# Full-size matmuls in a convolution made of Fourier transforms, and another order of its steps on TensorE and VectorE

## The reference

```
def conformer_conv(x, w_pw1, b_pw1, w_dw, b_dw, ln_g, ln_b, w_pw2, b_pw2):
    h = x @ w_pw1 + b_pw1                      # 1024 -> 2048
    a, gate = jnp.split(h, 2, axis=-1)
    h = a * jax.nn.sigmoid(gate)
    h = conv_general_dilated(h, w_dw, padding=[(30, 0)], feature_group_count=1024) + b_dw   # 31 taps, causal
    h = jax.nn.silu(layer_norm(h, ln_g, ln_b))
    return h @ w_pw2 + b_pw2                   # 1024 -> 1024
```

## Time and profile before

| | before |
|---|---|
| median of 3 runs | 1293.32 us (1292.26 to 1293.49) |
| profiled execution, its own time | 1291.84 us |
| its span in the profile | 1290.1 us |
| TensorE busy | 1266.2 us, 98% of the span |
| VectorE busy | 830.1 us, 64% |
| ScalarE busy | 611.7 us, 47% |
| mean granted TensorE clock | 0.999 |

### The profile page before, as it was taken

One profiled execution on the slowest core, in us unless ns is written; L12 is line 12 of the kernel. 1 busy time (PEld: TensorE's weight loads), 2 busy tenths in 40 slices (PEclk: granted clock), 3 DMA queues, 4 the chain that ended last, 5 costly groups with the idle time before them and its releaser, 6 DMA issues.

```text
span 1290.1 us, 16615 instructions
## 1 busy us (share of the span) xinstructions
PE 1266.2 (98%) x6802; PEld 1072.2 (83%) x6802; DVE 830.1 (64%) x953; ACT 611.7 (47%) x741; POOL 92.4 (7%) x126
## 2 busy tenths in 40 slices
PE   7999999999999999999999999999999999999997
PEld 5888877888988888768888889898888888988885
DVE  5556686767676655667676655567764666776663
ACT  4355567543455534435455533255553454555440
POOL 4123210100000002001000000000000110100000
PEclk9999999999999999999999999999999999999999
DMA  9655544465565566534655655556545413665540
GB/s 321 173 164 163 164 133 160 149 210 187 178 199 180 184 215 220 175 101 131 205 186 184 209 172 184 182 178 196 194 166 196 166 63 106 211 193 194 196 163 33
DMA packets 165067, 225.27 MB, mean 175 GB/s; under 512 B 7456, under 2 KB 105860, under 8 KB 164992
## 3 DMA queue, kind: packets, MB, share of 16 engines
q1 hardware_dynamic: 163168, 220.23, 52.6%
q0 software_dynamic: 1808, 3.98, 1.2%
q10 hardware_dynamic: 16, 0.00, 0.0%
HBM read 223.14 MB, written 1.05 MB: 174 GB/s over the span
## 4 chain that ended last, share of the span: by engine, by line
PE 95%; DVE 3%; ACT 1%; DMA 0%; issue 0%; POOL 0%; POOLq 0%; DVEq 0%; SPq 0%; ACTq 0%
PE acc L598 15%; PE acc L655 15%; PE acc L600 15%; PE acc L599 15%; PE att L655 8%; PE acc L653 8%; PE att L653 4%; PE acc L629 2%; PE acc L633 2%; PE acc L631 2%; PE tp L676 1%; DVE wlo L1365 1%; PE att L598 0%; ACT whi L1085 0%; PE att L599 0%; PE att L600 0%
## 5 line engine op out<-in xcount | busy, mean ns | idle before, releaser
L1365 DVE TENSOR_TENSOR wlo<-raw,whi 128x2048 fp32r<-128x2048 f32 x208 | 474.3, 2289 | 171.7 <-ACT whi L1085 171.2
L1085 ACT ACTIVATE whi<-raw 128x2048 fp32r<-128x2048 f32 x208 | 395.0, 1913 | 115.9 <-PE acc L600 105.7
L655 PE MATMUL acc<-aT,whi 128*128 128x512 f32 x832 | 291.0, 391 | 0.0
L653 PE MATMUL acc<-aT,wlo 128*128 128x256 f32 x832 | 233.6, 281 | 0.0
L655 PEld LDWEIGHTS acc<-aT,whi 128*128 128x128 f32 x832 | 155.6, 187 | 33.9
L598 PE MATMUL acc<-whi,aT 128*128 128x512 f32 x432 | 172.7, 400 | 2.0 <-DVE wlo L1365 2.0
L600 PE MATMUL acc<-wlo,aT 128*128 128x512 f32 x432 | 169.2, 392 | 0.0
L599 PE MATMUL acc<-whi,aT 128*128 128x512 f32 x432 | 169.1, 392 | 0.0
L655 PE MATMUL att<-aT,whi 128*128 128x512 f32 x448 | 157.8, 391 | 0.0
L653 PEld LDWEIGHTS acc<-aT,wlo 128*128 128x128 f32 x832 | 157.2, 189 | 0.0
L598 PE MATMUL acc<-whi,hT_hi 128*128 128x512 f32 x352 | 139.3, 396 | 0.0
(11 more groups left out here) (295 smaller groups left out, 1600.3 us busy)
## 6 DMA issues: line engine op xcount, KB each, us to landing
raw<-in_ffn_w_gate_dram SPq DMA_DIRECT2D x88, 512.0 KB, 4.0
raw<-in_ffn_w_up_dram SPq DMA_DIRECT2D x88, 512.0 KB, 5.2
raw<-in_ffn_w_down_dram SPq DMA_DIRECT2D x88, 512.0 KB, 4.8
raw<-in_w_in_dram SPq DMA_DIRECT2D x72, 512.0 KB, 4.8
raw<-in_conv_w_pw_dram SPq DMA_DIRECT2D x24, 512.0 KB, 4.8
raw<-in_w_kv_dram SPq DMA_DIRECT2D x16, 512.0 KB, 5.0
raw<-in_ret_w_o_dram SPq DMA_DIRECT2D x8, 512.0 KB, 4.6
raw<-in_diff_w_o_dram SPq DMA_DIRECT2D x8, 512.0 KB, 4.6
```

What stands on the lines that cost most here:

```text
L653: mm_(bank[:, 0:T], wlo[:, slot, cols], aT_hi[:, kt, :], start=half == 0 and j == 0, stop=False, skip_group_check=True)
L655: last = mm_(bank[:, :], whi[:, slot, cols], aT[:, kt, :, :].rearrange("p a n -> p (a n)"), start=False, stop=half == 1 and j == SLAB_K - ...
L1085: A_(whi[:, slot, :], raw[:, slot, :], ACT.Copy).then_inc(hi_ready, 1)
L1365: V.tensor_tensor(wlo[:, slot, :], raw[:, slot, :], whi[:, slot, :].bitcast(F32), ALU.subtract)\
```

## The change

There are three edits. First, `analyse` takes both row tiles at 128 columns of the table and the halo with all 128 rows; the table holds zeros where the padding reads. Second, on TensorE the first `make_tokens` waits for `prod_done` 4 alone, with the wait for 8 behind it, and the transposes of `yn` (0, 0) are issued between the two matmuls of the last `make_tokens`. Third, on VectorE the statistics of (1, 1) come after one `conv_low` and no longer after four, and the split `low(p2a.k + 3)` of the last `pw2` slab comes after `normalise(1, 1)`, where it came before `normalise(1, 0)`.

```
--- before.py
+++ after.py
@@ -891,19 +891,19 @@
                     pe.wait_ge(prod_done, 2 * (c - 1))
                 banks = [att, tp][c % 2]
                 cols = slice(c * FW, (c + 1) * FW)
-                halo = slice(P - 32, P)
-                for half, rows_ in ((0, SPEC_A), (1, SPEC_B)):
-                    to = slice(half * P, half * P + rows_)
-                    mm_(banks[half][0:rows_, 0:FW], own_tokens[:, to], u[:, 0, cols], start=True, stop=True)
-                    mm_(banks[half][0:rows_, FW:CW], own_tokens[:, to], u[:, 1, cols], start=True, stop=False)
-                    last = mm_(banks[half][0:rows_, FW:CW], last_tokens[halo, to], u[halo, 0, cols],
-                               start=False, stop=True)
+                for half in range(2):
+                    to = slice(half * P, (half + 1) * P)
+                    mm_(banks[half][:, 0:FW], own_tokens[:, to], u[:, 0, cols], start=True, stop=True)
+                    mm_(banks[half][:, FW:CW], own_tokens[:, to], u[:, 1, cols], start=True, stop=False)
+                    last = mm_(banks[half][:, FW:CW], last_tokens[:, to], u[:, 0, cols], start=False, stop=True)
                 last.then_inc(fwd_mm, 1)
 
-            def make_tokens(t, n):
+            def make_tokens(t, n, between=None):
 
                 cols = slice(n * CW, (n + 1) * CW)
                 mm_(y_banks(t)[n][:, :], back[:, 0:P], spec[:, 0, t, cols], start=True, stop=False)
+                if between:
+                    between()
                 mm_(y_banks(t)[n][:, :], back[0:SPEC_B + 1, P:2 * P], spec[0:SPEC_B + 1, 1, t, cols],
                     start=False, stop=True).then_inc(inv_mm, 1)
 
@@ -939,13 +939,13 @@
             analyse(2)
 
             analyse(3)
-            pe.wait_ge(prod_done, 8)
+            pe.wait_ge(prod_done, 4)
             pe.wait_ge(acc_free, 2 * (p1.g + 3) + 2)
             make_tokens(0, 0)
+            pe.wait_ge(prod_done, 8)
             make_tokens(0, 1)
             make_tokens(1, 0)
-            transpose_y(0, 0)
-            make_tokens(1, 1)
+            make_tokens(1, 1, lambda: transpose_y(0, 0))
             transpose_y(0, 1)
 
             for half in range(2):
@@ -1776,14 +1776,15 @@
             normalise(0, 0)
             normalise(0, 1)
             conv_stats(1, 0)
-            for kt in range(4):
-                conv_low(0, kt)
+            conv_low(0, 0)
             conv_stats(1, 1)
             conv_variance(1)
-            low(p2a.k + 3)
+            for kt in range(1, 4):
+                conv_low(0, kt)
             dve.wait_ge(yrs_ready, 1)
             normalise(1, 0)
             normalise(1, 1)
+            low(p2a.k + 3)
             for kt in range(4, KT):
                 conv_low(0, kt)
             for kt in range(KT):
```

## The result

| | before | changed |
|---|---|---|
| median of the runs | 1292.88 us (6 runs) | 1286.41 us (6 runs, 1285.91 to 1287.37) |
| ratio, 95% interval | | 0.9949 (0.9939 to 0.9959) |
| profiled execution, its own time | 1291.84 us | 1287.37 us |
| its span | 1290.1 us | 1285.6 us |
| first `analyse` to second half of `pw2` | 46.79 us | 41.35 us |

The changed kernel is faster by 0.51%, which is 6.5 us between the medians; 5.35 us was the sum. The last line of the table is the stretch that the change touches: from the first L897 at 534.62 to the `pw2` matmul at 581.41 before, from 535.58 to 576.93 after. It lost 5.44 us. The rest of the difference is the subject of the first experiment.

The account below looks back on a forecast made before the run. TensorE, busy for 98% of the span, was the bound. Terms of 2.5 + 1.7 + 0.5 + 0.65 = 5.35 us took the profiled 1291.84 us to 1286.5; 1.48 us more gave 1288.0 us (own range 1286.9 to 1289.0, whole 1286.4 to 1290.6).

Parts of the forecast that it names:

- The padding: In the four `analyse`: full tiles remove the "issue" gaps around the 32-row products, 2.5 us (bounds 0 and 2.8).
- The first inverse ahead of the last spectra: After `analyse(3)`: `make_tokens(0, 0)` fills TensorE's wait for `multiply(3)`, 1.7 us (bounds 1.6 and 1.8).
- U: The start of the transposes of `yn` (0, 0) on TensorE, at 571.84 before.
- T: The moment at which `analyse(3)` has been issued on TensorE, 564.04 before.
- Transposes inside the last inverse: Before `pw2`: less inverse work behind the transposes lets `pw2` start earlier, 0.5 us of 0.86 (bounds 0.4 and 0.86).
- The gap in the middle of `pw2`: Between the halves of `pw2`: token tile 1's transposes no longer wait, 7.00 us becomes 6.35, 0.65 us.
- with the split moved away: At GpSimd's two steps for token tile 1: without VectorE's slab split beside them, both take 0.9 us.
- The median of the runs is 1.48 us above it: Last step of the forecast: from 1286.5 us for the profiled execution to a median of 1288.0 us.
- GpSimd slow by itself: Rival at GpSimd's first step: slow without the split, TensorE waits 1.5 us at `pw2`'s second half, 1289.5 us; chance 0.13.
- Padded loads exposed: Rival in `analyse`: padded halo loads cost what they save, 2.4 us over all four, 1290.4 us; chance 0.07.
- Both steps held: Rival on GpSimd: both steps at 2.16 + 2.64 us, 3.5 us lost, 1291.5 us; chance 0.06.
- the split as the bound: Slower rival at `pw2`'s second half: late slab split holds TensorE, 8.2 us lost, 1296.2 us; chance 0.03.

Follow-up runs that it names:

- the first experiment: The kernel before and the changed kernel, each run again without an edit: 1292.30 us (0.9998) and 1286.26 us (0.9950).
- the last experiment: Kernel before with an unused one-input sum in the slab split's place and the split behind `normalise(1, 1)`: 1294.44 us, ratio 1.0008.

## Why the prediction was right, and where it was off

The forecast of 1288.0 us is 1.6 us above the measured 1286.41 us, which lies 0.5 us below the forecast's own range (1286.9 to 1289.0) and on the lower edge of the whole one (1286.4 to 1290.6). The mechanisms and their sum held; the step that failed is the one from the profiled execution to the median.

**The padding, 2.5 us.** Right in mechanism, too small: 2.73 us alone, and 2.90 us if it is taken out of the changed kernel (44.27 less 41.37). The two between slabs gave more than the 0.63 us counted for each. From the start of `analyse(0)` to the second L598 behind it there are now 3.29 us (535.58 to 538.87), and in the timeline of before 4.02 us (534.62 to 538.64): 0.73 us less. The term had stopped at the first L598 and put 2.60 us in front of it, where it starts after 2.41 us. What the prediction called padding of both tiles was in truth the rows alone; the 128 columns gave nothing.

**The first inverse ahead of the last spectra, 1.7 us.** Right: U at T + 6.07 as forecast, and 1.62 us by the experiment.

**Transposes inside the last inverse, 0.5 us.** Right: 0.43 us. `pw2` began at U + 2.18 where U + 2.08 was forecast, held by `conv_low(0, 0)` as forecast.

**The gap in the middle of `pw2`, 0.65 us.** Right in size: from start to start 6.32 us (570.61 to 576.93) after 7.00. The experiment puts VectorE's order at 0.90 us, because in the changed kernel TensorE comes to the transposes earlier, and the held GpSimd would cost more there. The step failed in one cause: it said that GpSimd is free "with the split moved away". The move of the split isn't needed (41.37 us without it); the statistics taken earlier are. GpSimd's step 0.32 us, `yrs` at U + 3.94, `conv_low(0, 4)` over at U + 7.91 are at the early end of the ranges forecast, or just ahead of it. The rule of the Trainium skill ("SBUF — State Buffer", Who interferes with whom) agrees with the 2.12 us beside a two-input instruction and the 0.19 us beside a one-input one. Its counterpart, that VectorE is held when GpSimd came first, is not seen: the split of 2.28 us that starts inside GpSimd's second step (570.86, step from 570.61 to 571.18) is no longer than others (2.24 to 2.29).

**The sum and the median: the step that failed.** The sum of 5.35 us stands against 5.44 us in the trace. What failed is the last step, "The median of the runs is 1.48 us above it". It took one profiled execution and three runs as if their distance belonged to the kernel. Its result before rounding, 1287.97 us, is 1.56 us above the measured median, and that divides in three. 0.44 us are the median of before: three runs gave 1293.32, six give 1292.88, and the larger sets 1292.48 to 1292.91. 0.09 us are the sum. 1.03 us lie in no stretch of the traces: the median less the convolution is 1246.09 us before and 1245.06 us after. How much of the 1.03 us is the spread of the first 20 us, how much goes with the lower granted clock in 27 of the 64 runs of before, and whether a part belongs to the program, stays open.

**The rivals.** GpSimd slow by itself: refuted by 0.19 us after a pause of 63.74 us. Padded loads exposed: refuted by the pace. Both steps held, and the split as the bound: neither came in this kernel. A split that is too late was made in the last experiment; it cost TensorE 1.64 us, and with the kernel's other waits it gave 1.0008, not clear of no change.

## What to carry to other kernels

A small matmul among full ones can cost more than a padded one, as 32 rows among 128 did here: read the starts of the matmuls around it, not the list of waits, since the gap is booked as "issue". When a small step on GpSimd is on the path, start it before VectorE's long instruction with two SBUF inputs, or put a one-input instruction there. And take a forecast of a few microseconds as a difference of traces over the changed stretch; the median of three runs less one profile, 1.48 us here, was no property of the kernel.

## What the hardware showed that was not expected

- 128x108 beside 128x128 costs nothing (0.43 us per product through the change), while 32 rows beside 128 cost 0.34 us there and back. Nor does every other number of rows cost: L907 with 109 rows between L904 with 128 starts 0.86 us before the next, as L904 does before it (562.37, 563.22, 564.09, 564.95 in the changed kernel).
- The products of `analyse_taps`, with 31 rows each, start in pairs 0.02 us apart, and each of the four reads other rows of the operands (`taps[32 * q:32 * q + 31]`, q from 0 to 3). The first four start within 0.34 us; four full ones, 0.43 us apart, start within 1.3. Small tiles among themselves were fast; it is the step to the full size that costs. The changed kernel's timeline of the first four:

```profile
523.48 0.48 PE L881 MATMUL att<-taps,table 31*128 31x256 f32 x2
523.50 0.48 PE L881 MATMUL tp<-taps,table 31*128 31x256 f32 x2
...
523.82 0.38 PE L881 MATMUL tp<-taps,table 31*128 31x256 f32 x2
```
